# The last expert of a mixture-of-experts layer in another order, and a finish stage that shares its additions differently between TensorE and VectorE

## What is computed

```
def expert_block(args):
    xb, e = args
    return (jax.nn.silu(xb @ w_gate[e]) * (xb @ w_up[e])) @ w_down[e]
...
out = jnp.zeros((t, d), F32).at[tok_buf].add(y_buf.astype(F32) * w_buf[:, None])
...
h = h + hierarchical_moe(...)
return rmsnorm(h, final_norm)
```

## Time and profile before

| | |
|---|---|
| median of 3 runs | 2177.26 (2175.57 to 2178.42) |
| profiled execution, its own time | 2172.84 |
| span of the profile | 2171.1 |
| TensorE (PE) matmuls busy | 2077.2, 96% |
| VectorE (DVE) busy | 1620.9, 75% |
| ScalarE (ACT) busy | 1340.6, 62% |
| mean granted clock of TensorE | 0.988 |

### The profile page before, as it was taken

How to read it: one execution, slowest core, us unless ns; L and a number is a source line. 1 busy time by engine, 2 the same in 40 slices (tenths; PEclk the granted TensorE clock), 3 DMA queues, 4 the chain that set the end, 5 groups by cost and what they waited for, 6 DMA issues and landing times. The chain is left out here.

```text
span 2171.1 us, 30452 instructions
## 1 busy us (share of the span) xinstructions
PE 2077.2 (96%) x10800; PEld 1710.5 (79%) x10800; DVE 1620.9 (75%) x1984; ACT 1340.6 (62%) x1671; POOL 233.0 (11%) x252
## 2 busy tenths in 40 slices
PE   8999998888999999999999979998799999999998
PEld 6778886777788888888877867887678888888885
DVE  4561246667888888888885276775798888888886
ACT  5332426553787887878862256553378788887884
POOL 1200000001211111111003310000211111111100
PEclk9999999999999999999999999999999999999999
DMA  4112322114999999999971020002599999999996
GB/s 135 39 58 79 85 78 80 68 59 169 353 385 383 391 389 384 379 378 384 385 288 74 1 88 11 11 21 80 177 351 380 381 386 384 387 388 385 384 370 249
DMA packets 123458, 513.28 MB, mean 236 GB/s; under 512 B 27357, under 2 KB 28458, under 8 KB 89578
## 3 DMA queue, kind: packets, MB, share of 16 engines
q1 hardware_dynamic: 103642, 474.09, 58.0%
q0 software_dynamic: 18576, 33.86, 4.1%
q10 hardware_dynamic: 1152, 4.19, 0.5%
HBM read 495.03 MB, written 50.86 MB: 251 GB/s over the span
## 5 line engine op out<-in xcount | busy, mean ns | idle before, releaser
L525 DVE TENSOR_TENSOR exp_w_lo<-ring_raw,first_w_hi 128x2048 fp32r<-128x2048 f32 x192 | 438.8, 2287 | 36.4 <-ACT first_w_hi L452 36.4
L525 DVE TENSOR_TENSOR exp_w_lo<-ring_raw,exp_w_hi 128x2048 fp32r<-128x2048 f32 x192 | 438.8, 2287 | 31.5 <-ACT exp_w_hi L452 31.5
L452 ACT ACTIVATE exp_w_hi<-ring_raw 128x2048 fp32r<-128x2048 f32 x192 | 367.7, 1917 | 60.3 <-PE exp_up_out L377 34.8
L452 ACT ACTIVATE first_w_hi<-ring_raw 128x2048 fp32r<-128x2048 f32 x188 | 360.8, 1919 | 59.8 <-PE exp_up_out L377 33.6
L377 PE MATMUL exp_y_out<-exp_w_lo,exp_hid_hi 128*128 128x512 f32 x512 | 200.3, 391 | 0.0
L377 PE MATMUL exp_gate_out<-exp_w_lo,exp_x_hi 128*128 128x512 f32 x512 | 200.3, 391 | 0.0
L377 PE MATMUL exp_up_out<-exp_w_lo,exp_x_hi 128*128 128x512 f32 x512 | 199.2, 389 | 0.0
L322 POOL DMA_INDIRECT y_rows<-exp_y,base_rows_y x63 | 72.6, 1152 | 968.6 <-ACT exp_y L472 953.0
L377 PE MATMUL exp_gate_out<-first_w_hi,exp_x_hi 128*128 128x512 f32 x272 | 109.2, 401 | 3.1 <-issue 2.0
L377 PEld LDWEIGHTS exp_up_out<-exp_w_lo,exp_x_hi 128*128 128x128 f32 x512 | 96.1, 188 | 19.8
L377 PEld LDWEIGHTS exp_gate_out<-exp_w_lo,exp_x_hi 128*128 128x128 f32 x512 | 96.3, 188 | 19.0 <-issue 0.2
(11 more groups left out here) (508 smaller groups left out, 4759.3 us busy)
## 6 DMA issues: line engine op xcount, KB each, us to landing
ring_raw<-in_expert_w_gate_dram SPq DMA_DIRECT2D x128, 1024.0 KB, 10.9
ring_raw<-in_expert_w_up_dram SPq DMA_DIRECT2D x128, 1024.0 KB, 11.2
ring_raw<-in_expert_w_down_dram SPq DMA_DIRECT2D x128, 1024.0 KB, 11.1
l0w_raw<-in_ab_w_in_dram SPq DMA_DIRECT2D x48, 256.0 KB, 2.8
finish_y<-y_rows SPq DMA_DIRECT2D x8, 1024.0 KB, 13.0
ring_raw<-in_swa_w_qkv_dram SPq DMA_DIRECT2D x5, 1024.0 KB, 9.9
ring_raw<-y_rows SPq DMA_DIRECT2D x10, 512.0 KB, 5.1
base_h<-in_x_dram ACTq DMA_DIRECT2D x8, 512.0 KB, 6.8
```

The costliest lines, as they stand in the source:

```text
L452: nc.scalar.activation(split[split_slot(unit)][0][:], raw[raw_slot(unit)][:], ACT.Copy).then_inc(hi_ready, 1)
L525: nc.vector.tensor_tensor(lo[:], raw[raw_slot(unit)][:], hi[:].bitcast(F32), ALU.subtract).then_inc(lo_ready[split_slot(unit)], 1)
```

## The change

Four edits, all in layer 1's last expert and in the finish stage. (1) The down product of expert 30 now stands between gate and up of expert 31, and SyncE loads the units in that order. ScalarE copies it before the high part of the last unit instead of after it; VectorE makes the low part of the last unit before silu times up instead of after it. (2) VectorE adds five row halves (both of tiles 0 and 1, the first of tile 2) in `vector_early`, and one (the first of tile 7) right ahead of that tile's combine; TensorE takes both halves of tiles 3 to 6 and one of tiles 2 and 7. (3) TensorE begins with the rows of tiles 2 and 3, and runs the rows of tile t + 2 ahead of the last expert's product of tile t; the accumulator is (t - 2) mod 4, and the 14 transposes ahead of the stage are gone. (4) The loads of y6 and y7 wait for the up product's last unit, and each combine has a drain ahead of it.

```diff
 # experts: sync
+            if weighted:
+                for half in range(2):
+                    load((last_pair, 2 + half), w_down[E - 2, half])
+                for half in range(2):
+                    load((last_pair, 4 + half), w_up[E - 1, half])
 # experts: tensor
-            gate_up(E - 1, (last_pair, 0))
-            down_of(E - 2, (last_pair, 4))
+            if weighted:
+                pe.wait_ge(x_cols_s, E)
+                pe.wait_ge(hid_ready, E)
+                for half in range(2):
+                    multiply((last_pair, half), (x_hi, x_lo), 4 * half, 4, [gate_out[:]], half == 0, half == 1)
+                down_of(E - 2, (last_pair, 2))
+                for half in range(2):
+                    multiply((last_pair, 4 + half), (x_hi, x_lo), 4 * half, 4, [up_out[:]], half == 0, half == 1)
 # experts: scalar
-            for u in range(5, 8):
-                make_hi((last_pair, u))
-            copy_y(E - 2, 0, (last_pair, 5))
+            if weighted:
+                make_hi((last_pair, 5))
+                make_hi((last_pair, 6))
+                copy_y(E - 2, 0, (last_pair, 3))
+                make_hi((last_pair, 7))
 # experts: vector
-            silu_times_up(E - 1, (last_pair, 3))
-            make_lo((last_pair, 7))
+            if weighted:
+                make_lo((last_pair, 7))
+                silu_times_up(E - 1, (last_pair, 5))
 # finish
-    T, ACC, both = 8, 4, (2, 4, 6)
+    T, ACC, EARLY, both = 8, 4, 2, (3, 4, 5, 6)
...
                 if t < 6:
                     before.until_slot_read(sp, t)
+                else:
+                    before.until_last_unit(sp, 5)
...
             def rows(t):
-                if t == 0:
-                    for k in range(14):
-                        at = BANK + (k % 4) * P
-                        nc.tensor.transpose(acc[3][:, at:at + P], c["ident"][:], c["ident"][:])
+                if t == EARLY:
                     pe.wait_ge(diag_made, 1)
                 if t >= ACC:
                     pe.wait_ge(combined, t - ACC + 1)
...
+            rows(EARLY)
+            rows(EARLY + 1)
             for t in range(T):
-                rows(t)
+                if t >= EARLY and t + 2 < T:
+                    rows(t + 2)
                 last_rows(t)
...
+        def add_rows(dve, t, k):
+            dve.wait_ge(y_ready[t], 16)
+            nc.vector.scalar_tensor_tensor(h[:, t], y[t][:, k], weight[:, k, t:t + 1], h[:, t], ALU.mult, ALU.add)
+
         def vector_early(dve):
-            pass
+            for t in range(EARLY):
+                add_rows(dve, t, 0)
+                dve.drain()
+                add_rows(dve, t, 1)
+            add_rows(dve, EARLY, 0)
...
             def combine(t):
+                if t == T - 1:
+                    add_rows(dve, t, 0)
+                dve.drain()
                 dve.wait_ge(summed, t + 1)
```

More of the change, by code:

```diff
@@ L311, in sync @@
                     gate_of(e + 1, pair, 6 * q + 6)
-            up_then_down(E - 1, last_pair, 2)
+            if weighted:
[4 more added lines that the diff above has]
+            else:
+                up_then_down(E - 1, last_pair, 2)
             for half in range(2):
@@ L439, in tensor @@
                     turn_hid(e)
-            gate_up(E - 1, (last_pair, 0))
-            down_of(E - 2, (last_pair, 4))
+            if weighted:
[6 more added lines that the diff above has]
+                    multiply((last_pair, 4 + half), (x_hi, x_lo), 4 * half, 4, [up_out[:]], half == 0, half == 1)
+            else:
+                gate_up(E - 1, (last_pair, 0))
+                down_of(E - 2, (last_pair, 4))
             turn_hid(E - 1)
@@ L504, in scalar @@
             silu_of(E - 1, (last_pair, 1))
-            for u in range(5, 8):
-                make_hi((last_pair, u))
-            copy_y(E - 2, 0, (last_pair, 5))
+            if weighted:
[3 more added lines that the diff above has]
+                make_hi((last_pair, 7))
+            else:
+                for u in range(5, 8):
+                    make_hi((last_pair, u))
+                copy_y(E - 2, 0, (last_pair, 5))
             hid_high(E - 1)
@@ L605, in vector @@
                 make_lo((last_pair, u))
-            silu_times_up(E - 1, (last_pair, 3))
-            make_lo((last_pair, 7))
+            if weighted:
+                make_lo((last_pair, 7))
+                silu_times_up(E - 1, (last_pair, 5))
+            else:
+                silu_times_up(E - 1, (last_pair, 3))
+                make_lo((last_pair, 7))
             hid_low(E - 1)
@@ L3115, in rows @@
                         cols = slice(b * BANK, (b + 1) * BANK)
-                        mm(acc[t % ACC][:, cols], diag[:, t, k], y[t][:, k, cols], start=(k == 0 or t not in both), stop=False)
+                        mm(acc[(t - EARLY) % ACC][:, cols], diag[:, t, k], y[t][:, k, cols], start=(k == 0 or t not in both), stop=False)
             def last_rows(t):
@@ L3120, in last_rows @@
                     before.until_last_rows(pe)
-                before.multiply_last(t, [acc[t % ACC][:, 0:BANK], acc[t % ACC][:, BANK:]], False).then_inc(summed, 1)
+                before.multiply_last(t, [acc[(t - EARLY) % ACC][:, 0:BANK], acc[(t - EARLY) % ACC][:, BANK:]], t < EARLY).then_inc(summed, 1)
+            rows(EARLY)
+            rows(EARLY + 1)
             for t in range(T):
-                rows(t)
+                if t >= EARLY and t + 2 < T:
+                    rows(t + 2)
                 last_rows(t)
@@ L3128, in scalar_early @@
             before.until_last_unit(act, 5)
-            for t in range(T):
+            for t in range(EARLY, T):
                 for k in (0, 1) if t in both else (1,):
@@ L3146, in vector @@
         def vector(dve):
[L3147 to L3151, removed]
             def combine(t):
+                if t == T - 1:
+                    add_rows(dve, t, 0)
+                dve.drain()
                 dve.wait_ge(summed, t + 1)
-                nc.vector.tensor_tensor(h[:, t], h[:, t], acc[t % ACC][:], ALU.add).then_inc(combined, 1)
+                nc.vector.tensor_tensor(h[:, t], h[:, t], acc[(t - EARLY) % ACC][:], ALU.add).then_inc(combined, 1)
             def normed(t):
@@ L3163, in normed @@
                 nc.vector.scalar_tensor_tensor(h[:, t], h[:, t], scale[:, t:t + 1], gain[:], ALU.mult, ALU.mult).then_inc(made, 1)
-            rows(0)
-            rows(1)
             combine(0)
             for t in range(T):
-                if t + 2 < T:
-                    rows(t + 2)
                 if t + 1 < T:
```

## The result

| | before | after |
|---|---|---|
| median of 9 runs each, side by side | 2177.26 us (2171.99 to 2178.66) | 2182.23 us (2177.08 to 2183.19) |
| profiled execution | 2172.84, span 2171.1 | 2183.01, span 2181.0 |
| mean granted clock of TensorE | 0.988 | 0.982 |

A forecast was written before the change was run, and what follows sets the result against it. Bound: expert 30's down product, copy, scatter and y loads, then TensorE through tile 7. Despite earlier loads the new finish stage ends 4.3 us later, plus 0.5 for the scatter: 4.8, so 2182.0 us, range 2179.0 to 2185.5.

The forecast's parts named there:

- The sum: Last expert and finish stage together: VectorE's end 4.3 us later, before 0.5 is added for a slower scatter.
- Early copy: Last expert: ScalarE copies expert 30's y at 2120.2 instead of 2125.63, so scatter and y loads come 5.4 us earlier.
- The scatter: Scatter of expert 30's y, ahead of the y loads: 0.5 us slower beside the gain load, bounds 0 and 1.5.
- Five early additions: VectorE's row additions and low half of the last rows end at 2138.4, before TensorE asks at 2141.8: free.
- TensorE's order: TensorE's ten row halves for eleven, starting on tile 2, waiting for y3 and ahead of tile 4: end 0.6 us earlier.
- rival C: Finish stage: y3 lands sooner, ending TensorE's wait between tiles 2 and 3; 2180.8 us, not tellably slower; chance 0.36.
- rival B: TensorE's clock falls after its gap ahead of tile 2's rows, losing 1.7 us; +6.5, 2183.8 us; chance 0.16.
- VectorE's tail: Last tiles: VectorE takes 2.7 us a tile, starts tile 7's combine at 2166.8 and ends at 2171.1.
- A: The forecast itself: +4.8 us; 2181.6 to 2183.8 us with the scatter's bounds and 0.7 for joints; chance 0.44.
- the joints: Allowance of 0.7 us in the forecast's own range for where its terms join.

The follow-up runs named there:

- e5: The changed kernel with the load of the final gain moved from ahead of the y loads to between y3 and y4; median 2180.78 us, ratio 1.0025.
- e8: The kernel before with only the last expert's new order on all engines, y6 and y7 waiting for up, and the old finish stage; 2175.02 us, ratio 1.0000.
- the second trace: The changed kernel run once more with no edit; median 2181.33 us, ratio 1.0028 against the kernel before.
- e4: The changed kernel with VectorE's addition of tile 7's first half moved ahead of tile 4's combine; median 2179.30 us, ratio 1.0018.
- e10: The changed kernel with tile-by-tile closing, 24 filler transposes, tile 7's addition early and the gain load behind y3; 2172.88 us, ratio 0.9992.
- e6: The last expert's new order, no fillers, TensorE in the old tile order with ten row halves, VectorE adding the other halves; 2173.90 us, ratio 0.9990.
- e9: The changed kernel with TensorE closing tiles 0, 1 and 2 right behind tile 2's rows, then going tile by tile; 2177.72 us, ratio 1.0012.
- e2: The changed kernel's finish stage behind the old order of the last expert; median 2186.18 us, ratio 1.0054 against the kernel before.

## Why the prediction was right

The time, its direction and its main mechanism came out as forecast: 2182.23 for 2182.0. One step was rated wrong, the clock. That the median lies within 0.2 all the same is in part luck: in the traces the tail grew by 6.2 and 6.0, where the forecast had 4.8, and the medians of the two measurements differ from before by 5.0 and 5.7, each known only to some 2 us. Also, the profiled span was 9.9 longer, not the 4 to 5 that the prediction named, 3.6 of it ahead of the change.

- **The sum, with the clock apart.** e5 is the changed kernel without the scatter's delay and, in its trace, without the fall: its tail is 4.4 longer than before, for a sum of 4.3, and TensorE ends 52.7 behind the gate where before had 53.2, 0.5 earlier for a forecast 0.6.
- **Early copy, and free by itself.** Copy at 2120.19 (2120.2), loads issued at 2125.80 (2125.7 with the scatter term), y2 at 2136.26 (2136.1 with it), last product ended at 2134.20 (2134.1), all on the scale of before. e8 shows that with the finish of before 0.4 of the 5.4 us by which the copy comes sooner reaches the tail.
- **The scatter.** 0.60 for a taken 0.5; e5 gives 0.50 of it back, which shows the cause. The prediction read "DMA: Bandwidth & Descriptors", section "Queues, rings and completion order", of the Trainium skill as a delay near 0; that reading is too low here by those 0.5 to 0.6 us, with the gain load in its way. Between 2127.59 and 2129.38, the scatter's last 1.8 us, the DMA engines were busy at 0.92 and more, where they had been at 0.22 to 0.28 under the scatter of before.
- **Five early additions free.** Yes: they end at 2141.2, the low half of the last rows at 2142.5, and tile 3's products run until 2147.3.
- **TensorE's order.** The stall ahead of tile 4 was 0.40 and 0.27 to fill up again (0.35 and 0.3). Without the clock's fall, in e5, the wait for y3 was 0.47 (0.5), so rival C's early y3 did not come: y3 was as late as interpolated.
- **The clock.** Here a step failed: rival B was given 0.16, "against it: one of 1.6 did not, and the new one is 1.5". The new gap was 2.20. The prediction had left its own 0.5 of the scatter out of that number, and the issue ahead of the first product (0.14). B is what both traces of the changed kernel show: a tail of +6.2 and +6.0, where B had +6.5. Whether some unprofiled executions keep their clock in the gap isn't settled; two of nine ran at a mean clock of 0.986 in 2177.1 and 2178.2, the others at 0.982 to 0.985 in 2180.9 to 2183.2, but the mean over the kernel doesn't tell: the second trace, at 0.987, has the fall.
- **VectorE's tail.** 2.75 a tile for 2.7, 3.93 for the one with the addition, and the combine of tile 7 5.0 after TensorE's end ("4.5 to 5"). The addition's place is 1.1 of the tail (e4).
- **The range of A.** Its lower bound, 2181.6, is the sum of 4.3 without the 0.7 for the joints; with them it would be 2180.9, which belongs to C.
- **What the size rests on.** The prediction put TensorE's small gain to its beginning "with tile 2 and then tile 3 instead of tile 0". The start on tile 2 does not by itself make the kernel slower than before: e10 keeps it. What it costs against a start on tile 0 was not tested alone; e6, with such a start and the same ten row halves, closes its last tile 49.5 behind the gate, and e10 52.1, but e6 also divides the halves otherwise. The costly thing is that tiles 0 and 1 are closed only behind tile 3's rows and that each tile's rows go two tiles ahead: 4.2 of the tail, most of it through VectorE, which is idle first and overloaded last.

Together: 4.2 (order of closing), 1.7 (scatter and the clock that fell with it), 1.1 (tile 7's addition), 7.0 in all against a loss of 6.1 in the tail; the 0.9 between is what the change brings once they are mended. It is the 1.0 of e10 once more and not a second measurement, and no run shows which part of the change gives it.

## What to carry to other kernels

Bringing data forward is worth what the next stage waited for it: y loads 4.8 to 4.9 us earlier were worth 0.4 in front of a finish that had waited 0.31 for tile 0, and 4.6 in front of one that had waited 7.58 for tile 2. When work moves from one engine to another, look at the order in which tiles are closed as much as at the sums: close each tile as soon as it can be, so that the next engine's share is spread, and put unwaited work where that engine is idle. When a gap's length decides something, work it out with every delay that the forecast itself assumes.

## What the runs showed of the hardware

- TensorE's clock after short gaps: after 1.54 us of idle time it stayed at 1.00 (e5, one trace); after 2.20 and 2.21 (the changed kernel), 2.31 (e9) and 2.17 (e4) it was still 1.00 at the first products and then 0.50 for some 3.4 us, while TensorE worked. By estimate, half a microsecond of delay on a scatter so cost 1.2 more on TensorE (1.7 of tail in e5, less the 0.5).
- In e2 the gap was 7.58 and the clock fell within it, as its stretches show:

```profile
2138.00:2140.00 2.00, 0.00 (x0) 0.00 (x0) 1.43 (x2) 0.00 (x0) 0.00 (x0) 0.50 0.98 414
...
2144.00:2145.00 1.00, 1.00 (x4) 0.39 (x3) 0.00 (x0) 0.00 (x0) 0.00 (x0) 0.83 1.11 459
```

  The low stretch was some 6.8 us long there, but about half of it lay in the gap. The twelve products then took 7.00, no more than after the gap of 2.20 (7.29): for them the longer gap was no dearer.
- A scatter of 0.5 MB took 3.19 (before, e2) to 3.30 (e5) with no load on the way beside it, and 3.79 to 3.88 (the changed kernel, e4, e9) with a load of 0.5 MB beside it in its last microseconds.
